# Gate products of the merge stage: three products per weight block run together, their weight sums kept on the chip, operand loads issued by ScalarE

## The chip, the cores and the metric

The kernel runs on one core of one Trainium2 chip. The metric is the time of one execution on the device in microseconds (us). Three runs of the kernel before the change gave 2289.18, 2292.55 and 2293.31 us, median 2292.55 us.

## What is computed

The program is one layer of a hybrid decoder: an input projection, an mLSTM and a sparse attention beside each other, a gated merge of the two, an output projection, cross-attention and a feed-forward block. Only the merge is touched. With `T` = 1056 tokens (1024 of a prompt and 32 of samples) and 1024 channels it is, cut to what matters:

```python
gates = sigmoid(h @ w_gate_m), sigmoid(h @ w_gate_n)      # two gates of 1024 channels
merged = gates[0] * (hm @ w_up_m) + gates[1] * (on @ w_up_n)
```

`h` is the normalised layer input, `hm` the mLSTM's output and `on` the attention's.

## The kernel before, in words

**The gate products.** `merge` (L2237) computes the gate logits by a seven-product scheme for 2x2 blocks (Strassen's in Winograd's form) instead of eight plain products. The weights of each gate are cut into eight blocks `j` of 128 output channels (`N_GATE` = 8; `j // 4` picks the gate), each block into four quarters of 128x512 numbers. The tokens are cut into two halves of 528. The seven products are numbered 1 to 7. Product 1 and 2 use a quarter as it is, 7 the difference of two quarters, 5 the sum of two quarters, 6 is product 5's sum less a third quarter, 3 is the fourth quarter less product 6's sum, 4 a quarter as it is. So 5, 6 and 3 build on each other's weight sums.

**Units.** A unit is one product for one block: 24 fp32r matmuls of 128x128 by 128x264. There are 7 x 8 = 56 units. `GATE_ORDER` is (1, 2, 7, 5, 6, 4, 3): all eight blocks of product 1, then all eight of product 2, and so on. `merge_uses` lists the uses of weights: two of the branch projection (`"m", 0` and `"m", 1`), the 56 units, then the other 14 of the branch projections, which are called late.

**The way of a weight.** For each use, SyncE's queue loads a raw tile (six slots: four `mg_raw`, two in `ring`), VectorE adds or subtracts two quarters if the product wants a sum (`weight_sum`, L2577), ScalarE copies the high part to one of five weight buffers `mg_w` (`weight_high`, L2493), GpSimd forms the low part (L69), and TensorE multiplies. Each product of numbers is three matmuls of high and low parts (`split_product`, L88). A weight buffer is free when the unit that read it is done, so ScalarE can copy at most the weights four units ahead of the one that runs.

**Sums in DRAM.** The raw slots can't hold a sum from product 5 to product 6, eight units later. So SyncE writes each sum of products 5 and 6 to DRAM (`keep_sum`, L2381, tensor `gate_sums`) before it reuses the slot, and loads it again, beside one more quarter, for product 6 (L2368, L2369) and product 3 (L2373, L2374). The reuse of a slot waits on the write (`kept`).

**Operands.** Each product has its own token operand (`B_SOURCE`: from `h_t` or `h_spill` in DRAM, 1056 KB). Three operand buffers `mg_b` rotate. SyncE loads the raw form (`load_b`, L2349) when the product three before is done; ScalarE forms its high part in two pieces (`b_high`, L2509) and VectorE its low part in two (`b_low`, through L69). All of it stands in one order on each engine, written out by the loop over the units.

**Results.** ScalarE copies the results of products 1, 7 and 5 out of PSUM (`keep`, L2504), VectorE adds the others into `mg_za` and `mg_zb` (`evac`, L2593 to L2612). A PSUM pair is free four units later. `gate` (L2514) applies the sigmoid, VectorE then multiplies with the branch projections (`weigh`, L2630).

Of the kernel before, what the change touches and what calls it, by code (L numbers as in the profile page):

```python
# [2222 lines left out]
GATE_ORDER = (1, 2, 7, 5, 6, 4, 3)  # L2223
GATE_QUADS = {1: slice(1, 2), 2: slice(0, 1), 7: slice(1, 3), 5: slice(2, 4), 6: slice(1, 2), 4: slice(3, 4), 3: slice(0, 1)}
N_PAIR, N_GATE = 4, 8


def merge_uses():

    uses = [("m", 0), ("m", 1)] + [(p, j) for p in GATE_ORDER for j in range(N_GATE)]  # L2230
    uses += [("n", 0), ("n", 1)]
    for c in range(2, KD):
        uses += [("m", c), ("n", c)]
    return uses


def merge(nc, A, hm, on, low_at, z_at, b_at, w_at, end, ring, dst_high, dst_low, out_half, tile_at, split_at, psum):  # L2237
# [17 lines left out]
    raw_slot = [4, 4, 5, 5] + [(v - 4) % 6 for v in range(4, LATE)] + [(v - LATE) % 4 for v in range(LATE, NU)]  # L2255
    before = lambda slots, v: max((u for u in range(v) if slots[u] == slots[v]), default=None)
    w_before = [before(w_slot, v) for v in range(NU)]
    raw_before = [before(raw_slot, v) for v in range(NU)]
    parts_of = lambda v: 2 if uses[v][0] in (6, 3) else 1
    raw_count, seen = {}, {}  # L2260
    for v in range(4, NU):
        seen[raw_slot[v]] = seen.get(raw_slot[v], 0) + parts_of(v)
        raw_count[v] = seen[raw_slot[v]]
    kept_count, seen = {}, {}
    for v in range(NU):
        if uses[v][0] in (5, 6):
            seen[raw_slot[v]] = seen.get(raw_slot[v], 0) + 1
            kept_count[v] = seen[raw_slot[v]]
# [3 lines left out]
    Z_ACT = {(p, j): n * N_GATE + j + 1 for n, p in enumerate((1, 7, 5)) for j in range(N_GATE)}  # L2272
    Z_DVE, done = {}, 0
    for p, some in ((2, ("c11",)), (6, ("u2", "u3")), (4, ("u4", "c22", "c21")), (3, ("c12",))):
        for j in range(N_GATE):
            for what in some:
                done += 1
                Z_DVE[what, j] = done
    READ = {2: "c11", 6: "u2", 4: "c21", 3: "c12"}
    B_SOURCE = {1: (0, 0), 2: (4, 0), 3: (4, 1), 5: 0, 7: 1, 6: 2, 4: 3}  # L2280

    with stage(nc, "merge") as (ctx, sem):
# [8 lines left out]
        hm_high, on_high = split_at("mg_hm_high", [P, 4, T], b_at[1]), split_at("mg_on_high", [P, 4, T], b_at[2])  # L2291
# [6 lines left out]
        kept = [sem(f"kept{s}") for s in range(6)]  # L2298
# [4 lines left out]
        def source(v):  # L2303
            if v < 4:
                return raw[4 + v // 2][:, 512 * (v % 2):512 * (v % 2) + 512]
            return raw[raw_slot[v]][:, 0:512]
# [15 lines left out]
        def wait_raw(eng, v):  # L2322
            if v >= 4:
                eng.wait_ge(raw_loaded[raw_slot[v]], 16 * raw_count[v])
# [8 lines left out]
        GATE_READY = {(j // 4, 4 * m + j % 4): n * N_GATE + j + 1 for n, m in enumerate((1, 0)) for j in range(N_GATE)}  # L2333

        @block.sync
        def _(sp):
            def load_b(q):
                s, p = q % 3, GATE_ORDER[q]
                at = B_SOURCE[p]
                if q == 0:  # L2340
                    for k in range(4):
                        sp.dma_start(braw[0][:, k, :], A["h_spill"][:, k, 0:HN]).then_inc(b_first[k], 16)
                    return
                if q < 3:
                    sp.wait_ge(S["up"], 4)
                else:
                    sp.wait_ge(S["prod"], N_GATE * (q - 2))
                src = A["h_t"][at] if isinstance(at, int) else A["h_spill"][:, at[0]:at[0] + 4, half_cols(at[1])]
                sp.dma_start(braw[s][:, :, :], src).then_inc(b_loaded[s], 16)  # L2349

            def load_raw(v):
                u = raw_before[v]
# [4 lines left out]
                x, at = uses[v]  # L2357
                to, done = raw[raw_slot[v]], raw_loaded[raw_slot[v]]
# [4 lines left out]
                quads = A["w_gate"][at // 4, at % 4]  # L2363
                n = GATE_QUADS[x].stop - GATE_QUADS[x].start
                if x == 6:
                    w = unit_use(GATE_ORDER.index(5) * N_GATE + at)
                    sp.wait_ge(kept[raw_slot[w]], 16 * kept_count[w])
                    sp.dma_start(to[:, 0:512], A["gate_sums"][0, at]).then_inc(done, 16)  # L2368
                    sp.dma_start(to[:, 512:1024], quads[:, 1, :]).then_inc(done, 16)  # L2369
                elif x == 3:  # L2370
                    w = unit_use(GATE_ORDER.index(6) * N_GATE + at)
                    sp.wait_ge(kept[raw_slot[w]], 16 * kept_count[w])
                    sp.dma_start(to[:, 512:1024], A["gate_sums"][1, at]).then_inc(done, 16)  # L2373
                    sp.dma_start(to[:, 0:512], quads[:, 0, :]).then_inc(done, 16)  # L2374
                else:
                    sp.dma_start(to[:, 0:512 * n].rearrange("p (q w) -> p q w", q=n), quads[:, GATE_QUADS[x], :]).then_inc(done, 16)
# [6 lines left out]
            load_b(0)  # L2383
            for v in range(4, 8):
                load_raw(v)
            b_at_use = {11: 1, 13: 2}
            for q in range(3, 7):
                b_at_use[N_GATE * (q - 2) + 14] = q
            for v in range(8, LATE):
                if v in b_at_use:  # L2390
                    load_b(b_at_use[v])
                if v >= 10 and v - 6 in kept_count:
                    keep_sum(v - 6)
                load_raw(v)
            for v in range(LATE, LATE + 4):
                load_raw(v)
# [3 lines left out]
            for v in range(LATE + 4, NU):  # L2400
                load_raw(v)
            sp.wait_ge(S["ahead_loaded"], 32)
# [9 lines left out]
        def _(pe):  # L2412
            def up(v, q, x):
                w = wt[w_slot[v]]
                for h in range(2):
                    for c in range(2):
                        g = 2 * h + c
                        if v < FIRST:
                            pe.wait_ge(S["hm_first_low"], g + 1)
                        for k in range(4):  # L2420
                            ks = slice(k * P, (k + 1) * P)
# [7 lines left out]
            def unit(n):  # L2429
                v = unit_use(n)  # L2430
                p, j = uses[v]
                q, s = n // N_GATE, n // N_GATE % 3
# [6 lines left out]
                for c in range(2):  # L2439
                    for k in range(4):  # L2440
                        if n == 0 and c == 0:
# [42 lines left out]
        def _(act):  # L2484
            def weight_high(v):
                wait_raw(act, v)
                if v in sum_count:
                    act.wait_ge(S["w_sum"], sum_count[v])
                if w_before[v] is not None:
# [10 lines left out]
            def keep(n):  # L2500
                p, j = uses[unit_use(n)]
                act.wait_ge(S["prod"], n + 1)
                f, h = {1: (j % 4, 1), 7: (4 + j % 4, 0), 5: (4 + j % 4, 1)}[p]
                nc.scalar.activation(cols(z[j // 4][:, f, half_cols(h)]), pair(n % 4), ACT.Copy).then_inc(S["z_act"], 1)  # L2504
# [19 lines left out]
            for g in range(4):  # L2524
                nc.scalar.activation(bt[1 + g // 2][:, 0, :, col(g % 2)], hm[:, :, col(g)], ACT.Copy).then_inc(S["hm_first_high"], 1)
# [7 lines left out]
            keep_early(1)  # L2533
            weight_high(5)
            for n in range(UNITS):
# [4 lines left out]
                if uses[unit_use(n)][0] in (1, 7, 5):  # L2540
                    keep(n)
                if q < 6 and j in (3, 4):
                    b_high(q + 1, j - 3)
                if q == 6:
                    if j == 0:
                        gate(N_GATE - 1, 1)
                    else:
                        gate(j - 1, 0)
                    if j < 4:
                        other_high(on_high, on, j, N_GATE * 6, "on_high")  # L2550
                    else:
                        other_high(hm_high, hm, j - 4, N_GATE * 5, "hm_high")
                if q == 5 and j:
                    gate(j - 1, 1)
            weight_high(LATE + 2)
            gate(N_GATE - 1, 0)
# [12 lines left out]
        def _(ve):  # L2569
            tt = nc.vector.tensor_tensor  # L2570

            def weight_sum(v):
                x, j = uses[v]
                wait_raw(ve, v)
                w = raw[raw_slot[v]]
                a, b = w[:, 0:512], w[:, 512:1024]
# [2519 lines left out]
```

## Time and profile before

| what | value |
|---|---|
| median of three runs | 2292.55 us (2289.18 to 2293.31) |
| the profiled execution's own time | 2294.28 us |
| its span in the profile | 2292.1 us |
| granted clock of TensorE, mean | 0.968 of full speed |
| TensorE busy | 2166.3 us, 95% of the span |
| VectorE, ScalarE, GpSimd busy | 1355.2, 906.7, 640.8 us |
| the merge stage's matmuls | 840.30 us to 1121.08 us in the span |

Times in the views are microseconds from the start of the span. L88 is the line of every split matmul, L69 that of every low part; there the tile names (`mg_...`) tell the stage. SPq and ACTq are the queues from which SyncE and ScalarE issue DMAs. A clock of 1.00 is TensorE's upper level of 2.4 GHz, 0.50 is 1.2 GHz.

### The profile page before, as it was taken

What the parts mean: (1) busy time and instruction counts of PE and PEld (TensorE: products, weight loads), DVE (VectorE), ACT (ScalarE), POOL (GpSimd) and SP (SyncE); (2) the same over time, 40 slices, a digit from 0 to 9 for tenths busy, and PEclk for the clock granted to TensorE, in tenths of its full rate; (3) what the DMA queues carried; (4) which work ended last, traced back from release to release, by engine and by line L of the source; (5) the groups of instructions that cost most, each with busy time, mean ns of one, the idle gap of its engine ahead of it and who ended that gap; (6) DMA issues with size and microseconds to landing.
All of it is one profiled execution on the core that took longest, in us unless ns stands there. A gap on an engine that the chain in (4) does not pass through costs nothing. (4 is left out here: it accounts for less than half of the span.)

```text
span 2292.1 us, 44079 instructions
## 1 busy us (share of the span) xinstructions
PE 2166.3 (95%) x17491; PEld 1982.6 (86%) x17491; DVE 1355.2 (59%) x2442; ACT 906.7 (40%) x1806; POOL 640.8 (28%) x562
## 2 busy tenths in 40 slices
PE   9999998989888989979999999999899999999997
PEld 7799977865555679979999988898899999999997
DVE  2323445256665664466428145657899887876957
ACT  4221244116655654343234133554333433334443
POOL 0000025412232214432111300132344433445643
PEclk9999999879999999989999999999999999999998
DMA  4231187973453436551221146342223132265234
GB/s 152 105 116 47 36 156 243 308 280 112 139 167 93 146 118 214 168 170 56 83 87 37 38 187 238 122 140 84 89 94 117 72 121 89 85 234 186 91 120 147
DMA packets 147593, 302.87 MB, mean 132 GB/s; under 512 B 26211, under 2 KB 78084, under 8 KB 141693
## 3 DMA queue, kind: packets, MB, share of 16 engines
q1 hardware_dynamic: 124668, 258.77, 33.8%
q0 software_dynamic: 10368, 28.33, 3.9%
q10 hardware_dynamic: 12352, 12.96, 1.8%
q8 instruction: 139, 2.28, 0.4%
q14 instruction: 66, 0.53, 0.1%
HBM read 247.41 MB, written 56.78 MB: 133 GB/s over the span
## 5 line engine op out<-in xcount | busy, mean ns | idle before, releaser
L88 PE MATMUL psum<-mg_b,mg_w 128*128 128x264 f32 x1440 | 183.8, 291 | 18.9 <-DVE mg_b L69 10.2
L88 PEld LDWEIGHTS psum<-mg_b,mg_w 128*128 128x128 f32 x1440 | 182.6, 195 | 20.1 <-issue 17.6
L88 PE MATMUL psum<-merged_high,oq_half 128*128 128x352 f32 x768 | 188.7, 326 | 1.8 <-POOL oq_half L69 1.4
L88 PE MATMUL psum<-ff_t,ff_x_slots 128*128 128x264 f32 x1200 | 149.1, 284 | 1.4 <-DVE ff_x_slots L69 1.4
L88 PEld LDWEIGHTS psum<-ff_t,ff_x_slots 128*128 128x128 f32 x1200 | 147.1, 188 | 1.6 <-issue 1.5
L88 PEld LDWEIGHTS psum<-merged_high,oq_half 128*128 128x128 f32 x768 | 135.2, 190 | 2.5 <-POOL oq_half L69 1.9
L1662 POOL DMA_DIRECT2D na_kv<-in_pool x128 | 69.0, 539 | 230.8 <-PE psum L1869 160.3
L1967 ACT ACTIVATE na_pt<-psum 128x512 f32<-128x512 f32 (+1 forms) x170 | 86.6, 543 | 93.5 <-PE psum L1842 85.0
L88 PE MATMUL psum<-ff_bslot,ff_x_slots 128*128 128x264 f32 x888 | 117.8, 286 | 0.7 <-DVE ff_z L4599 0.7
L69 POOL TENSOR_TENSOR ff_x_slots<-low,ff_x_slots 128x512 fp32r<-128x512 f32 x52 | 82.2, 1594 | 113.8 <-ACT ff_x_slots L4047 108.9
L88 PEld LDWEIGHTS psum<-ff_bslot,ff_x_slots 128*128 128x128 f32 x888 | 112.5, 189 | 1.0 <-DVE ff_z L4599 0.9
L88 PE MATMUL psum<-ff_t,ff_slot 128*128 128x264 f32 x840 | 106.5, 287 | 5.8 <-DVE ff_bufs L4476 2.2
L88 PEld LDWEIGHTS psum<-ff_t,ff_slot 128*128 128x128 f32 x840 | 104.6, 191 | 6.4 <-DVE ff_bufs L4476 2.4
L1842 PEld LDWEIGHTS psum<-consts,na_p 128*128 128x128 f32 x528 | 59.7, 148 | 54.6 <-DVE na_p L2116 31.1
L69 POOL TENSOR_TENSOR mg_w<-mg_raw,mg_w 128x512 fp32r<-128x512 f32 x50 | 73.6, 1479 | 112.0 <-ACT mg_w L2493 111.9
L88 PE MATMUL psum<-ff_b,ff_x_slots 128*128 128x264 f32 x840 | 104.8, 284 | 0.0
L88 PEld LDWEIGHTS psum<-ff_b,ff_x_slots 128*128 128x128 f32 x840 | 103.2, 188 | 0.0
L88 PE MATMUL psum<-in_half,h_high 128*128 128x512 f32 (+3 forms) x360 | 101.0, 366 | 2.2 <-DVE in_half L69 2.2
L1947 ACT ACTIVATE na_p<-na_p,na_nm 128x640 f32<-128x640 f32 (+7 forms) x128 | 92.8, 727 | 25.7 <-DVE na_nm L1983 25.5
L88 PE MATMUL psum<-ff_b,ff_slot 128*128 128x264 f32 x744 | 97.5, 290 | 3.6 <-DVE ff_bufs L4486 2.1
L88 PE MATMUL psum<-x_half_high,ff_aw 128*128 128x264 f32 x512 | 96.9, 288 | 3.4 <-DVE h_again_low L69 3.4
L88 PEld LDWEIGHTS psum<-ff_b,ff_slot 128*128 128x128 f32 x744 | 94.6, 194 | 4.2 <-DVE ff_bufs L4486 2.5
(692 smaller groups left out, 5457.6 us busy)
## 6 DMA issues: line engine op xcount, KB each, us to landing
na_kv<-in_pool SPq DMA_DIRECT2D x128, 128.0 KB, 3.6
na_kv<-in_pool POOLq DMA_DIRECT2D x128, 128.0 KB, 4.2
ff_bslot_raw<-mid_ops SPq DMA_DIRECT2D x59, 264.0 KB, 3.2
mid_ops<-ff_bufs SPq DMA_DIRECT2D x11, 1056.0 KB
ring<-in_f_wu SPq DMA_DIRECT2D x11, 1024.0 KB, 5.3
low<-in_f_wg SPq DMA_DIRECT2D x22, 512.0 KB, 4.6
first_pages<-in_pool SPq DMA_DIRECT2D x68, 128.0 KB, 5.8
ff_wd<-in_f_wd SPq DMA_DIRECT2D x3, 2816.0 KB, 11.6
```

The costliest lines, as they stand in the source:

```text
L69: return engine.tensor_tensor(low, x, high.bitcast(F32), ALU.subtract)
L88: ins = nc.tensor.matmul(out, w[a], x[b], start=first and n == 0, stop=last and n == 2)
L1662: eng.dma_start(kv[m % 2][:, b, 2 * PAGE * p:2 * PAGE * (p + 1)], A["pool"][ds(g, 1), :, 2 * PAGE:4 * PAGE].rearrange("a p x -> (a p) x")) ...
L1842: last = nc.tensor.transpose(out[:, c:c + P], src, K["ident"][:, :])
L1947: ins = nc.scalar.activation(x, x, ACT.Exp, bias=nm[:, b, g, i:i + 1], scale=-1.0, accum_out=sums[:, b, g:g + 1])
L1967: nc.scalar.activation(dst, psum[:, 4 + n % 2, 0:2 * m * P], ACT.Copy).then_inc(S["copied"], 1)
```

## The change

It reorders the units: products 1 and 2 as before, then products 5, 6 and 3 mixed block by block (`SHARED`), then 7 and 4. The four quarters of a block come in two loads of 512 KB, "sums" and "last"; product 5's sum, product 6's and product 3's are formed in these two slots one after the other. `gate_sums` and its 16 writes and 16 reads are gone. The operand loads of all products but the first move from SyncE's queue to ScalarE's. Results are added in another order (ScalarE keeps products 1 and 5 alone, VectorE takes 7), VectorE forms the weight sums five units ahead instead of four, the sigmoids of the first gate half move to product 7's units, a product's first unit waits for its operand in two steps, and the very first operand piece is formed in two halves.

```diff
-GATE_ORDER = (1, 2, 7, 5, 6, 4, 3)
+GATE_ORDER = (1, 2, 5, 6, 3, 7, 4)
+SHARED = [(p, j) for j in range(3) for p in (5, 6)] + [(3, 0), (3, 1)]
+SHARED += [x for j in range(3, 6) for x in ((5, j), (6, j), (3, j - 1))]
+SHARED += [(5, 6), (5, 7), (6, 6), (6, 7), (3, 5), (3, 6), (3, 7)]
+GATE_QUADS = {1: slice(1, 2), 2: slice(0, 1), 7: slice(1, 3), 4: slice(3, 4), "sums": slice(2, 4), "last": slice(0, 2)}
...
+def merge_loads(uses):
+    loads, seen = [], set()
+    for v in range(4, len(uses)):
+        p, j = uses[v]
+        if p not in (5, 6, 3):
+            loads.append(uses[v])
+        elif j not in seen:
+            seen.add(j)
+            loads += [("sums", j), ("last", j)]
+    return loads
...
+    first_parts = [(0, slice(0, 2)), (0, slice(2, 4)), (1, slice(0, 4)), (2, slice(0, 4)), (3, slice(0, 4))]
...
+            def load_raw(n):
+                x, at = loads[n]
+                u = load_before[n]
                 if u is not None:
-                    if u in kept_count:
-                        sp.wait_ge(kept[raw_slot[u]], 16 * kept_count[u])
-                    wait_w_low(sp, u)
+                    p, j = loads[u]
+                    if p == "sums":
+                        wait_w_low(sp, use_of[6, j])
+                        sp.wait_ge(S["w_sum"], sum_count[use_of[3, j]])
+                    else:
+                        wait_w_low(sp, use_of[3, j] if p == "last" else use_of[p, j])
...
-            def keep_sum(v):
-                x, j = uses[v]
-                sp.wait_ge(S["w_sum"], sum_count[v])
-                sp.dma_start(A["gate_sums"][0 if x == 5 else 1, j], raw[raw_slot[v]][:, 0:512]).then_inc(kept[raw_slot[v]], 16)
...
-                        elif j == 0 and k == 0:
-                            pe.wait_ge(S["b_low"], 4 + 2 * q)
+                        elif j == 0 and c == 0 and k % 2 == 0:
+                            pe.wait_ge(S["b_low"], 4 + 2 * (q - 1) + k // 2 + 1)
...
+            def load_b(q):
+                s, p = q % 3, GATE_ORDER[q]
+                at = B_SOURCE[p]
+                if q < 3:
+                    act.wait_ge(S["up"], 4)
+                else:
+                    act.wait_ge(S["prod"], unit_of[GATE_ORDER[q - 3], N_GATE - 1] + 1)
+                src = A["h_t"][at] if isinstance(at, int) else A["h_spill"][:, at[0]:at[0] + 4, half_cols(at[1])]
+                act.dma_start(braw[s][:, :, :], src).then_inc(b_loaded[s], 16)
...
+            b_load_at, b_high_at = {9: 3, 17: 4, 35: 5, 38: 6}, {3: 1, 10: 2, 13: 3, 19: 4, 37: 5, 43: 6}
             for n in range(UNITS):
                 q, j = divmod(n, N_GATE)
                 v = n + 6
                 if v < LATE + 2:
                     weight_high(v)
-                if uses[unit_use(n)][0] in (1, 7, 5):
+                if GATE_UNITS[n] in Z_ACT:
                     keep(n)
-                if q < 6 and j in (3, 4):
-                    b_high(q + 1, j - 3)
+                if n in b_load_at:
+                    load_b(b_load_at[n])
+                if n in b_high_at:
+                    b_high(b_high_at[n], 0)
+                if n - 1 in b_high_at:
+                    b_high(b_high_at[n - 1], 1)
+                if q == 5:
+                    gate(j, 0)
...
             for n in range(UNITS):
                 q, j = divmod(n, N_GATE)
-                v = unit_use(n + 4)
+                v = unit_use(n + 5)
                 if v in sum_count:
                     weight_sum(v)
                 evac(n)
...
-           "h_t": (4, P, 4, T // 2), "gate_sums": (2, 8, P, 512)}
+           "h_t": (4, P, 4, T // 2)}
```

SyncE's queue before, in the middle of product 5's and 6's units (`mg_b_raw_13002` is the raw operand of one product, 128x2112 numbers; `mg_raw_...` and `ring` are raw weight slots):

```order
L2368 DMA mg_raw_12986<-gate_sums 128x512
L2369 DMA mg_raw_12986<-in_w_gate 128x512
L2349 DMA mg_b_raw_13002<-h_t 128x2112
L2381 DMA gate_sums<-ring 128x512
L2368 DMA ring<-gate_sums 128x512
L2369 DMA ring<-in_w_gate 128x512
L2381 DMA gate_sums<-ring 128x512
L2368 DMA ring<-gate_sums 128x512
```

The same queue now, in the units of products 5, 6 and 3:

```order
L2376 DMA mg_raw_12985<-in_w_gate 128x1024
L2376 DMA mg_raw_12986<-in_w_gate 128x1024
L2376 DMA ring<-in_w_gate 128x1024 x2
L2376 DMA mg_raw_12983<-in_w_gate 128x1024
L2376 DMA mg_raw_12984<-in_w_gate 128x1024
```

A write, a read of a sum and a load of a quarter per unit, with an operand load among them, have become loads of 512 KB alone, two for three units.

ScalarE's order now, in the units around product 3's first one (`mg_w_...` are weight buffers, `mg_b_12998` and `mg_b_raw_13001` product 3's operand, L2500 its load):

```order
L2479 ACTIVATE mg_w_12991<-mg_raw_12983 128x512
L2500 DMA mg_b_raw_13001<-h_spill 128x4x528
L2479 ACTIVATE mg_w_12992<-mg_raw_12986 128x512
L2490 ACTIVATE mg_za<-psum 128x528
L2479 ACTIVATE mg_w_12988<-ring 128x512
L2505 ACTIVATE mg_b_12998<-mg_b_raw_13001 128x1056
L2479 ACTIVATE mg_w_12989<-mg_raw_12985 128x512
L2490 ACTIVATE mg_za<-psum 128x528
L2505 ACTIVATE mg_b_12998<-mg_b_raw_13001 128x1056
```

The operand's load (issued from SyncE before) now stands between ScalarE's weight copies, and its two high parts follow behind it in the same order.

## Rows read from the trace of the kernel before

**Rows 1.** The page's head and section 1: span, then busy time by engine.

```profile
span 2292.1 us, 44079 instructions
PE 2166.3 (95%) x17491; PEld 1982.6 (86%) x17491; DVE 1355.2 (59%) x2442; ACT 906.7 (40%) x1806; POOL 640.8 (28%) x562
```

**Rows 2.** Windows: stretch, length, busy us (instructions) of PE PEld DVE ACT POOL, clock, DMA, GB/s.

```profile
858.00:873.00 15.00, 15.00 (x125) 15.00 (x125) 2.52 (x2) 7.59 (x12) 8.01 (x6) 1.00 0.54 182
873.00:890.00 17.00, 17.00 (x142) 17.00 (x141) 3.37 (x5) 5.14 (x8) 7.23 (x6) 1.00 0.72 248
...
1008.00:1023.00 15.00, 9.48 (x58) 9.31 (x57) 11.13 (x16) 8.71 (x11) 7.41 (x5) 0.77 0.31 99
```

**Rows 3.** TensorE's waits, 836 to 1126 us: total, times, longest.

```profile
PE psum L88 <- DVE mg_b L69: 10.2, 3, 5.5
PE psum L88 <- POOL mg_w L69: 8.7, 4, 5.1
```

**Rows 4.** Timeline of TensorE, gate products: start, length, idle before and its releaser.

```profile
840.30 121.25 PE L88 MATMUL psum<-mg_b,mg_w 128*128 128x264 f32 x984 [3.32 <-DVE mg_b L69]
...
977.40 11.90 PE L88 MATMUL psum<-mg_b,mg_w 128*128 128x264 f32 x96 [1.34 <-DVE mg_b L69]
994.44 13.76 PE L88 MATMUL psum<-mg_b,mg_w 128*128 128x264 f32 x96 [5.14 <-POOL mg_w L69]
1013.72 25.96 PE L88 MATMUL psum<-mg_b,mg_w 128*128 128x264 f32 x192 [5.52 <-DVE mg_b L69]
1039.52 0.28 PE L88 MATMUL psum<-mg_on_high,mg_w 128*128 128x264 f32 x1
```

**Rows 5.** Timeline of ScalarE: copies of product 1's first and eighth result.

```profile
856.70 0.61 ACT L2504 ACTIVATE mg_za<-psum 128x528 f32<-128x528 f32 x1 [1.26 <-PE psum L88]
...
877.10 0.61 ACT L2504 ACTIVATE mg_zb<-psum 128x528 f32<-128x528 f32 x1 [1.79 <-PE psum L88]
```

**Rows 6.** Windows of TensorE alone, after the last long wait: length, busy, clock, DMA.

```profile
1014.00:1017.00 3.00, 3.00 (x15) 0.50 0.15 57
```

**Rows 7.** Timeline of SyncE's queue, issues around two of the operand loads.

```profile
942.53 0.32 SPq L2349 DMA_DIRECT2D mg_b_raw<-h_t  x1
942.91 0.42 SPq L2381 DMA_DIRECT2D gate_sums<-ring  x1
951.01 0.32 SPq L2368 DMA_DIRECT2D ring<-gate_sums  x1
...
980.59 0.43 SPq L2349 DMA_DIRECT2D mg_b_raw<-h_spill  x1
981.07 0.50 SPq L2381 DMA_DIRECT2D gate_sums<-mg_raw  x1
989.26 0.33 SPq L2376 DMA_DIRECT2D mg_raw<-in_w_gate  x1
```

**Rows 8.** DMAs, issues of 836 to 1126 us: KB each, median us to landing.

```profile
mg_raw<-in_w_gate SPq DMA_DIRECT2D x10, 512.0 KB, 5.0
mg_b_raw<-h_t SPq DMA_DIRECT2D x4, 1056.0 KB, 7.7
```

**Rows 9.** DMAs, issues of 879 to 890 us: the slowest landings of 512 and 1056 KB.

```profile
mg_b_raw<-h_t SPq DMA_DIRECT2D x1, 1056.0 KB, 8.6
mg_raw<-in_w_gate SPq DMA_DIRECT2D x2, 512.0 KB, 6.5
```

**Rows 10.** Tiles mg_raw, mg_b: ns min/median/max of one, first and last start.

```profile
L2493 ACT ACTIVATE mg_w<-mg_raw x50: 612/623/636, 849.0 to 1101.5; 128x512 fp32r<-128x512 f32 x50
L69 POOL TENSOR_TENSOR mg_w<-mg_raw,mg_w x50: 1262/1294/2297, 850.4 to 1102.9; 128x512 fp32r<-128x512 f32 x50
L2577 DVE TENSOR_TENSOR mg_raw<-mg_raw x20: 677/692/1786, 889.4 to 1019.9; 128x512 f32<-128x512 f32 x20
L69 DVE TENSOR_TENSOR mg_b<-mg_b_raw,mg_b x16: 696/1255/2352, 845.7 to 1012.0; 128x1056 fp32r<-128x1056 f32 x12, 128x528 fp32r<-128x528 f32 x4
L2509 ACT ACTIVATE mg_b<-mg_b_raw x12: 1066/1076/1078, 866.0 to 1003.4; 128x1056 fp32r<-128x1056 f32 x12
```

More of the change, by code:

```diff
@@ L2264, in merge @@
[L2264 to L2268, printed above, removed]
+    loads = merge_loads(uses)
+    late_load = loads.index(uses[LATE])
+    load_slot = [n % 6 for n in range(late_load)] + [(n - late_load) % 4 for n in range(late_load, len(loads))]
+    load_before = [before(load_slot, n) for n in range(len(loads))]
+    load_count = [load_slot[:n + 1].count(load_slot[n]) for n in range(len(loads))]
@@ L2269, in merge @@
+    load_of = {}
+    for v in range(4, NU):
+        p, j = uses[v]
+        load_of[v] = loads.index(("sums", j) if p in (5, 6) else ("last", j) if p == 3 else (p, j))
     summed = [v for v in range(NU) if uses[v][0] in (7, 5, 6, 3)]
     sum_count = {v: n + 1 for n, v in enumerate(summed)}
-    Z_ACT = {(p, j): n * N_GATE + j + 1 for n, p in enumerate((1, 7, 5)) for j in range(N_GATE)}
+    use_of = {x: v for v, x in enumerate(uses)}
+    unit_of = {x: v - FIRST for v, x in enumerate(uses)}
@@ L2273, in merge @@
+    kept_units = [x for x in GATE_UNITS if x[0] in (1, 5)]
+    Z_ACT = {x: n + 1 for n, x in enumerate(kept_units)}
     Z_DVE, done = {}, 0
[L2274 to L2279, printed above, removed]
+    for p, j in GATE_UNITS:
+        for what in {1: (), 2: ("c11",), 5: (), 6: ("u2", "u4"), 3: ("c12",), 7: ("u3", "c22"), 4: ("c21",)}[p]:
+            done += 1
+            Z_DVE[what, j] = done
@@ L2297, in merge @@
         raw_loaded = [sem(f"raw_loaded{s}") for s in range(6)]
-        kept = [sem(f"kept{s}") for s in range(6)]
         b_first = [sem(f"b_first{k}") for k in range(4)]
@@ L2362, in load_raw @@
                     return
[L2363 to L2376, printed above, removed]
-            def keep_sum(v):
-                x, j = uses[v]
-                sp.wait_ge(S["w_sum"], sum_count[v])
-                sp.dma_start(A["gate_sums"][0 if x == 5 else 1, j], raw[raw_slot[v]][:, 0:512]).then_inc(kept[raw_slot[v]], 16)
[L2383 to L2396, printed above, removed]
+                quads = A["w_gate"][at // 4, at % 4][:, GATE_QUADS[x], :]
+                some = GATE_QUADS[x].stop - GATE_QUADS[x].start
+                sp.dma_start(to[:, 0:512 * some].rearrange("p (q w) -> p q w", q=some), quads).then_inc(done, 16)
+            for k in range(4):
+                sp.dma_start(braw[0][:, k, :], A["h_spill"][:, k, 0:HN]).then_inc(b_first[k], 16)
+            for n in range(late_load + 4):
+                load_raw(n)
             for j in range(2):
@@ L2399, in _ @@
                 sp.dma_start(ring[:, j, :], A["w_out"][j]).then_inc(S["ahead_loaded"], 16)
-            for v in range(LATE + 4, NU):
-                load_raw(v)
+            for n in range(late_load + 4, len(loads)):
+                load_raw(n)
             sp.wait_ge(S["ahead_loaded"], 32)
@@ L2522, in part_high @@
                 nc.scalar.activation(dst_high[:, c, :], za[:, c, :], ACT.Copy).then_inc(S["parts_high"], 1)
-            for g in range(4):
-                nc.scalar.activation(bt[1 + g // 2][:, 0, :, col(g % 2)], hm[:, :, col(g)], ACT.Copy).then_inc(S["hm_first_high"], 1)
+            for g, ks in first_parts:
+                nc.scalar.activation(bt[1 + g // 2][:, 0, ks, col(g % 2)], hm[:, ks, col(g)], ACT.Copy).then_inc(S["hm_first_high"], 1)
             weight_high(2)
@@ L2572, in weight_sum @@
             def weight_sum(v):
[L2573 to L2576, printed above, removed]
-                tt(a, a, b, ALU.add if x == 5 else ALU.subtract).then_inc(S["w_sum"], 1)
+                p, j = uses[v]
+                if p == 6:
+                    first, last = (raw[load_slot[loads.index((x, j))]] for x in ("sums", "last"))
+                    ve.wait_ge(S["w_sum"], sum_count[use_of[5, j]])
+                    wait_load(ve, loads.index(("last", j)))
+                    tt(first[:, 512:1024], first[:, 0:512], last[:, 512:1024], ALU.subtract).then_inc(S["w_sum"], 1)
+                elif p == 3:
+                    first, last = (raw[load_slot[loads.index((x, j))]] for x in ("sums", "last"))
+                    ve.wait_ge(S["w_sum"], sum_count[use_of[6, j]])
+                    tt(last[:, 0:512], last[:, 0:512], first[:, 512:1024], ALU.subtract).then_inc(S["w_sum"], 1)
+                else:
+                    w = raw[load_slot[load_of[v]]]
+                    wait_load(ve, load_of[v])
+                    tt(w[:, 0:512], w[:, 0:512], w[:, 512:1024], ALU.add if p == 5 else ALU.subtract).then_inc(S["w_sum"], 1)
             def b_low(q, m):
@@ L2662, in _ @@
                 evac(n)
-                if q < 6 and j in (4, 6):
-                    b_low(q + 1, (j - 4) // 2)
+                if n in b_low_at:
+                    b_low(b_low_at[n], 0)
+                if n - 1 in b_low_at:
+                    b_low(b_low_at[n - 1], 1)
                 if q == 6 and 1 <= j <= 4:
```

110 lines of the change are left out of this document (47 added, 63 removed).

## The prediction

> **What bounds the kernel now.** I read the page's head first: TensorE is busy for 95% of a span of 2292.1 us [rows 1]. So only its idle time and its slow time can be won. The windows say where in the merge it is slow. From 858 to 890 us it does 125 matmuls in 15 us and 142 in 17, about 0.12 us each, at clock 1.00; from 1008 to 1023 only 58, at clock 0.77 [rows 2]. The list of TensorE's waits names two releasers, `mg_b` from VectorE for 10.2 us and `mg_w` from GpSimd for 8.7 us, 18.9 us together [rows 3].
>
> The timeline gives the stage's ideal. Product 1's first result is copied at 856.70 us and its eighth at 877.10, seven units later: a unit takes 2.914 us [rows 5]. Unit 0 thus began at about 853.8 us, and the last of the 56 ended at 1039.5, where the first `mg_on_high` matmul stands [rows 4]. That is 185.7 us; 56 units of 2.914 us are 163.2. **22.5 us are lost.** Of these 18.9 less the 3.32 us that stand before the first matmul, so 15.6 us, are idle [rows 3, 4]. The other 6.9 us are slow matmuls: after each long wait TensorE runs at 1.2 GHz for some time, 15 matmuls in 3 us at clock 0.50 where 25 are usual [rows 6].
>
> SyncE's queue shows what is late. At 942.53 us it issues an operand load, right behind it the write of a sum to DRAM, and the next read of a sum into that slot waits for this write until 951.01, 8.1 us later. The same again: operand load at 980.59, write at 981.07, next weight load at 989.26 [rows 7]. TensorE idles 5.14 us before 994.44 for that weight. The 5.52 us before 1013.72 are put down to the operand's low part [rows 4], but VectorE's low part stands in its order behind the weight sums, which wait for the reads of `gate_sums`. So nearly all comes from the round trip of the sums and from what stands behind it in an order.
>
> **The change, part by part.** I call E(n) the end of unit n.
>
> *Round trip removed.* 16 writes and 16 reads of 256 KB and the waits on them go. At most 22.5 us come back, at least 0. What is late next is either a weight or an operand, so I check both.
>
> *Weights in the mixed stretch.* A weight buffer is free at E(n-1) for unit n+4. ScalarE copies 0.62 us, GpSimd takes 1.29, at most 2.30 [rows 10]: ready by E(n-1)+2.9, needed at E(n+3), 11.7 us after E(n-1). The raw slot "last" of block 0 is free when unit 22's low part is done, at E(17)+2.9 at the latest. SyncE issues (0.4 us) and 512 KB land in 5.0, at most 6.5 us [rows 8, 9]: E(17)+9.8. Then sum, high and low part, at most 1.79+0.62+2.30: E(17)+14.5. Unit 25 needs it at E(24), which is E(17)+20.4. Later blocks have the same distance or more. Slack 6 us, so no stall: 0. Traffic: 1 MB per three units (8.7 us) is 120 GB/s, 512 KB per unit in product 7 is 180; the old stretch of product 7 moved 248 GB/s while TensorE never idled [rows 2].
>
> *Other engines.* Per three units VectorE has three sums (0.69) and three result additions (0.70): 4.2 of 8.7 us. GpSimd has 1.29 of 2.9. ScalarE loses eight result copies and gets six DMA issues of about 0.43 us. None is near its limit. The queue behind ScalarE's waits is its weight copies, which have 8 us of lead: cost 0. If that cover went, each microsecond would show on TensorE.
>
> *Operands.* Six loads go to ScalarE's order. Two are tight. Product 3's (needed by unit 22, second step 0.73 us after E(21)): its second high part follows the result copy of unit 20, so E(20)+0.6+1.07, then the low part 1.25, at worst 2.35 [rows 10]: ready at E(20)+2.9 to 4.0, needed at E(20)+3.6. Stall 0 to 0.4 us. Product 7's: issued just after E(34), lands 7.7, at most 8.6 us later [rows 8, 9]. Two high parts with a weight copy between them need 2.8 us, the low part 1.25 to 2.35, so done at 11.7 to 13.8 us after E(34). On VectorE it also stands behind the result of unit 38, which makes it E(38)+0.7+1.25 to 2.35, so 13.6 to 14.7. Needed at E(39)+0.7, which is 15.3. Slack 0.6 to 1.7 us; the load itself may take up to about 10.5 us. Stall 0 as shown, 3 us if it lands 3 us later than any did. I take 0.8 us for all operands together, near the lower end, since the rows' medians leave slack.
>
> The rows say that an operand load on SyncE's queue held up what stood behind it for 8 us [rows 7]. A second queue lets the weights go on beside it. The Trainium skill (DMA: Bandwidth & Descriptors, "Issuing engines are not separate DMA queues") speaks against a gain from this part: loads from ScalarE run on the same 16 engines and interleave, so only issue time is saved. By that rule the 1056 KB take as long as before and the weights beside them longer, and this part alone gives back about 0.4 us for each of six loads on SyncE, none of it on TensorE. My sum does not need the part: 22.5 us is the whole loss, from whatever queue.
>
> *The start.* The first operand piece is made in two halves, so ScalarE's 1.07 and VectorE's 1.25 us shrink to about 0.6 and 0.7 [rows 10] before the first matmul; but VectorE first splits a weight. The first matmul comes about 0.5 us earlier and the following pieces 0.1 later. Between 0 and 1.2 us; I take 0.3.
>
> *The end.* The 16 late products and the following stage find the same orders behind them, their rows show TensorE busy, and they move up with it: 0.
>
> **Sum:** 22.5 + 0.3 - 0.8 = 22.0 us. The profiled execution took 2294.28 us, so 2272.3 by its own measure. It stands 1.7 us above the median of 2292.55, so I forecast **2270.5 us** against the median. The likeliest case alone: from a loss of 3.5 us that stays (2273.5) to all 22.5, 1.2 at the start and a run on the low side by some 2 us (2267).
>
> **Rivals.** *A: a late operand takes the place (0.16).* Product 7's or product 3's load meets the weight loads on the other queue and lands after 11 us. For: 0.6 us of slack at worst. Against: none took over 8.6 us. Its price is that of the stretch from 1008 to 1023 us, where 58 matmuls took 15 us instead of 7: 8 us with the slow clock [rows 2]. Gain 14, **2278.5 us**. The page's rule points this way too.
>
> *B: weights stay late in part (0.11).* Waits that I put down to the round trip are in truth bandwidth: 512 KB loads then land late in the mixed stretch and in product 7's, and half the loss stays. Against: 248 GB/s went without a stall. Gain 11, **2281.5 us**.
>
> *C: slower (0.05).* ScalarE is one order: while it waits at its high part for an operand, the weight copies of all later units stand behind it. This decides once a load takes more than the 10.5 us and also eats the weights' lead of 8 us, so from about 19 us, over twice the slowest row. Then each of five loads stops TensorE for the 5.5 us seen at 1013.72 and slows it as there, 8 us each: 40 us lost, 22.5 won, **2310 us**.
>
> *D: the change does not do what it says (0.02).* The stalls come back at full length elsewhere in the stage, at the first wait for an operand or in what follows. **2292.5 us.**
>
> **How the numbers follow.** Forecast 0.66, A 0.16, B 0.11, C 0.05, D 0.02. About 0.2%, 4.6 us, is what a measurement of this kernel can tell from no change. Forecast, A and B are all faster by more: 0.93. Same 0.02, slower 0.05. The range goes from 2267 us to 2279.5, which takes in A and leaves out B, C and D, 0.18.
>
> **What would show it.** The list of waits in the merge has 4 to 5 us instead of 18.9, nearly all before the first matmul, and no entry over 1 us after it. The clock is 1.00 in every window from unit 4 to the end of the gate products. `mg_on_high` begins near 1017 us instead of 1039.5, and everything later is 22 us earlier. No `gate_sums` rows. `mg_b` loads of 1056 KB stand on ScalarE's queue and land in 7 to 9 us. Wrong would be: a wait for `mg_b` of over 2 us at unit 22 or unit 40 (A), waits for `mg_w` in the mixed units (B), ScalarE idle for long on a DMA of `mg_b_raw` with TensorE idle behind it (C), or a stage shorter by 22 us with the span not shorter by as much (D).

## The result and the profile after

| | before | after |
|---|---|---|
| median | 2292.93 us (2289.18 to 2294.81, 4 runs) | 2264.78 us (2262.45 to 2267.57, 4 runs) |
| profiled execution's own time, span | 2294.28, 2292.1 us | 2262.45, 2260.8 us |
| mean granted clock | 0.968 | 0.975 |
| merge's first matmul to the first `mg_on_high` matmul | 840.3 to 1039.5 us | 833.0 to 1009.8 us |

The ratio of the time after to the time before is 0.988, with an interval of 0.9862 to 0.9898: 23.4 to 31.6 us faster. The forecast was 2270.5 us, its range 2267 to 2279.5. The measured median lies 2.2 us below the range.

The page's head and section 1 of the kernel after, against [rows 1]: TensorE does the same 17491 matmuls in 14.5 us less of busy time, and its idle time shrinks too.

```profile
span 2260.8 us, 44015 instructions
PE 2151.8 (95%) x17491; PEld 1971.8 (87%) x17491; DVE 1359.1 (60%) x2443; ACT 904.5 (40%) x1799; POOL 646.7 (29%) x562
```

TensorE's waits after, 830 to 1126 us (total, times, longest), against [rows 3]:

```profile
PE psum L88 <- DVE mg_b L69: 2.7, 1, 2.7
PE psum L88 <- PEq L146: 0.3, 1, 0.3
```

Of 18.9 us one wait of 2.7 is left, and the timeline of TensorE shows that it stands before the first matmul. With the 0.3 us of the second row that is 3.0, where the prediction had 4 to 5. The six gaps inside the units before, of 0.4 to 5.5 us (three of them in [rows 4]), are gone; the row of 1435 matmuls (from a window that begins at 834 us, so inside the row above it) has no gap in it.

```profile
829.96 0.33 PE L1853 MATMUL psum<-consts,na_acc 128*128 128x128 f32 x1
833.03 17.17 PE L88 MATMUL psum<-mg_b,mg_w 128*128 128x264 f32 x124 [2.74 <-DVE mg_b L69]
...
833.72 176.23 PE L88 MATMUL psum<-mg_b,mg_w 128*128 128x264 f32 x1435
1009.79 0.28 PE L88 MATMUL psum<-mg_on_high,mg_w 128*128 128x264 f32 x1
```

ScalarE's timeline has the copy of an early result (`mg_early`) that is released as TensorE turns to unit 0, at 846.8 us. From there to 1009.8 are 163.0 us; 56 units of 2.914 us are 163.2. Nothing is lost in the units any more.

```profile
846.85 0.61 ACT L2484 ACTIVATE mg_early<-psum 128x528 f32<-128x528 f32 x1 [2.31 <-PE psum L88]
```

The windows say the same of the clock (columns as in [rows 2]): 1.00 everywhere but at the start, busy as long as the window is.

```profile
833.03:850.00 16.97, 16.92 (x124) 16.71 (x125) 8.58 (x10) 9.71 (x17) 6.74 (x5) 0.90 0.61 194
...
890.00:922.00 32.00, 32.00 (x266) 32.00 (x265) 26.80 (x26) 11.53 (x18) 19.88 (x12) 1.00 0.44 150
922.00:960.00 38.00, 38.00 (x315) 38.00 (x314) 26.97 (x28) 12.29 (x19) 20.96 (x14) 1.00 0.51 177
960.00:990.00 30.00, 30.00 (x250) 30.00 (x249) 22.43 (x27) 18.59 (x23) 15.05 (x11) 1.00 0.33 115
```

Where the rest of the 31.3 us between the two spans comes from needs more profiles than two. The experiments give eleven more, so one table stands here for all. "Stage" runs from the start of the last attention matmul (L1853) to the first `mg_on_high` matmul; "rest" from there to the end of the span. All in us.

| kernel | attention ends | stage | rest | span |
|---|---|---|---|---|
| before | 836.6 | 202.9 | 1252.6 | 2292.1 |
| before, again (`e1_before_again`) | 833.8 | 202.0 | 1252.7 | 2288.5 |
| `e5_before_operands_on_act` | 833.3 | 199.0 | 1255.0 | 2287.3 |
| `e11_before_low_first` | 834.1 | 200.0 | 1252.5 | 2286.6 |
| after | 830.0 | 179.8 | 1251.0 | 2260.8 |
| after, again (`e2_after_again`) | 832.8 | 179.8 | 1250.8 | 2263.4 |
| `e3_tensor_declared` | 836.1 | 179.8 | 1250.6 | 2266.5 |
| `e4_operands_on_sync` | 829.7 | 180.4 | 1252.5 | 2262.6 |
| `e6_write_sums_too` | 840.8 | 180.3 | 1249.9 | 2271.0 |
| `e7_start_whole` | 833.4 | 180.1 | 1252.1 | 2265.6 |
| `e8_keep_clock` | 832.2 | 179.8 | 1248.2 | 2260.2 |
| `e9_start_order` | 833.1 | 179.5 | 1251.2 | 2263.8 |
| `e10_start_order_and_clock` | 830.7 | 178.2 | 1252.4 | 2261.3 |

The stage gave 23.1 us in the first pair. Another 6.6 us come from before the merge, where the change touches nothing: the attention ends anywhere from 829.7 to 840.8 us, without regard to the kernel. Between these two extremes, `e4_operands_on_sync` and `e6_write_sums_too`, TensorE's busy time up to the attention's end differs by 9.5 us over as many matmuls, at a mean clock of 0.96 and 0.95, so most of the 11.1 us is slower matmuls and not waiting. The windows of the two (length, busy, clock, DMA, GB/s):

```profile
0.00:829.70 829.70, 768.32 (x6645) 0.96 0.47 148
0.00:840.80 840.80, 777.78 (x6644) 0.95 0.47 146
```

The last 1.6 us are in the rest. They too are a matter of the clock, at one place late in the feed-forward block. 384 matmuls there take 52.5 or 52.6 us in the four profiles of the old order and in that of `e10_start_order_and_clock`, where the clock is at 0.50 for 6.8 us of it, and 50.0 or 50.1 us in the eight others, where it stays at 1.00. In all thirteen TensorE has three short idle times of 0.6 to 0.9 us there. Windows of `before`, `after` and `e10_start_order_and_clock` (columns as above):

```profile
2175.50:2178.50 3.00, 3.00 (x15) 0.50 0.00 0
2145.80:2148.80 3.00, 3.00 (x27) 1.00 0.00 0
2144.90:2147.90 3.00, 3.00 (x16) 0.50 0.01 3
```

This accounts for the 2.2 us by which the rest is shorter on average in the new order (1251.0 against 1253.2): 2.5 us are lost in four of four profiles of the old order and in one of nine of the new. Why the clock fell in some and not in others isn't shown.

### The profile page after: what moved, and what is told of

Read it like the earlier page. It is cut to its first block and busy times, and to the rows that moved or that the text cites. A ratio compares the mean times of both kernels' runs of the same rounds, so it can differ in the third digit from the quotient of the medians.

```text
span 2260.8 us, 44015 instructions
## 1 busy us (share of the span) xinstructions
PE 2151.8 (95%) x17491; PEld 1971.8 (87%) x17491; DVE 1359.1 (60%) x2443; ACT 904.5 (40%) x1799; POOL 646.7 (29%) x562
## 5 line engine op out<-in xcount | busy, mean ns | idle before, releaser
L88 PE MATMUL psum<-mg_b,mg_w 128*128 128x264 f32 x1440 | 176.9, 286 | 2.8 <-DVE mg_b L69 2.7
L88 PEld LDWEIGHTS psum<-mg_b,mg_w 128*128 128x128 f32 x1440 | 176.5, 190 | 3.2 <-DVE mg_w L69 2.9
L69 POOL TENSOR_TENSOR mg_w<-mg_raw,mg_w 128x512 fp32r<-128x512 f32 x51 | 81.6, 1605 | 102.9 <-ACT mg_w L2479 102.8
```

The lines of the kernel that those rows point to most:

```text
L69: return engine.tensor_tensor(low, x, high.bitcast(F32), ALU.subtract)
L88: ins = nc.tensor.matmul(out, w[a], x[b], start=first and n == 0, stop=last and n == 2)
```

## Experiments

**The two kernels once more.** `e1_before_again` is the kernel before, `e2_after_again` the changed one, both without an edit.

> The kernel before, unchanged, as a measure of what two equal programs differ by and of how far the part ahead of the merge moves from one execution to the next. Theory L (luck): the 6.7 us by which the merge began earlier in the changed kernel's profile are spread of the attention stages' clock; then this kernel's merge begins anywhere between about 828 and 840 us, its gate products take 199 us again from first matmul to first late product, and the ratio is 1.000 within 0.002. Theory S (systematic): something in the changed program makes the unchanged stages faster; then the merge begins at 836 us or later here too.

Measured: 2291.9 us (2282.72 to 2298.99, 12 runs) against 2292.46 (2280.65 to 2299.07, 17 runs), ratio 1.0002 (0.9985 to 1.0019). Equal programs differ by up to 18 us between runs. TensorE's waits in this profile:

```profile
PE psum L88 <- DVE mg_b L69: 12.6, 3, 6.5
PE psum L88 <- POOL mg_w L69: 4.6, 5, 1.1
PE psum L88 <- DVE mg_za L2608: 0.9, 1, 0.9
```

The total is that of [rows 3] within 1 us, but its shares are others. Who is named at a wait is the last link of one loop, and not a cause by itself.

> The changed kernel, unchanged. Theory L: with more rounds the gain shrinks to that of the merge stage, 22.5 to 24 us, ratio 0.990, and the merge begins anywhere between 828 and 840 us. Theory S: the gain stays at 28 us, ratio 0.988, and the merge begins near 830 us as in the first profile. Both: 176.8 us from the first matmul of the merge to the first late product.

Measured: 2265.03 us (2264.00 to 2269.02, 6 runs), ratio 0.9892 (0.9868 to 0.9916), which is 24.8 us, interval 19.3 to 30.3; the two medians are 27.4 us apart. Both theories' ratios lie in the interval, so the time doesn't decide. The table does as to the stages ahead of the merge: they end between 829.7 and 840.8 us with the new order and between 833.3 and 836.6 with the old, and 840.8 is one of the changed ones. From the first matmul to the first late product there are 176.7 us, as expected. The stage gave 22.2 us in this pair.

**A layout of DRAM?** The tensor `gate_sums` is declared again and stays unused.

```diff
-           "h_t": (4, P, 4, T // 2)}
+           "h_t": (4, P, 4, T // 2), "gate_sums": (2, 8, P, 512)}
```

> The changed kernel with the DRAM tensor gate_sums declared but not used, so that DRAM is laid out as before. Theory S in the form that the layout of DRAM helps the other stages: the gain falls from 28 to about 22.5 us (ratio 0.990) and the merge begins at 836 us. Theory L: no different from the changed kernel within 2 us.

Measured: 2265.68 us (2261.88 to 2273.97), ratio 0.9895 (0.9866 to 0.9923), stage 179.8. The declaration changes nothing that these runs can tell.

**Operands back on SyncE's queue, in the new order.** `load_b` moves from ScalarE to SyncE unchanged but for the engine.

```diff
+            b_before = {7: 1, 9: 2, 16: 3, 20: 4, 35: 5, 37: 6}
...
+                if n in b_before:
+                    load_b(b_before[n])
...
-                if n in b_load_at:
-                    load_b(b_load_at[n])
```

> The changed kernel with the six operand loads back on SyncE's queue, before the weight loads that are released at about the same time. My theory, that the round trip was the loss and the second queue gives nothing of it: the same time within 2 us, no wait over 1 us for mg_b or mg_w in the units. Rival, that the second queue carries a good part of the gain since weights stood behind operand loads: weights land up to 8 us later at three places, and 5 to 12 us come back as waits for mg_w or mg_b.

Measured: 2267.97 us (2264.25 to 2271.07), ratio 0.9904 (0.9880 to 0.9928), stage 180.4. The second queue is worth 0.6 us of the stage here. The 2.9 us between this median and that of `e2_after_again` are not in any wait, and the intervals overlap.

**Operands on ScalarE's queue, in the old order.** The converse. The loads are issued once the product three before is done. That is also earlier than before, where they stand in SyncE's order: product 4's at 926.17 us instead of 942.53, product 3's at 955.23 instead of 980.59. So the edit moves both the queue and the time of the loads.

```diff
+            load_b(1)
             weight_high(5)
+            load_b(2)
...
+                if j == 1 and 1 <= q < 5:
+                    load_b(q + 2)
```

> The kernel before with one part of the change alone: its six operand loads issued by ScalarE; products in the old order, sums through DRAM as before. My theory, that the waits come from the round trip as such and from the order that puts a sum's write, read and use close together: at most a third of the loss goes, the merge's gate products still take over 190 us from the first matmul to the first late product (176.7 in the changed kernel, 198.3 to 199.2 before), with waits for mg_w and mg_b of over 10 us beside the start. Rival, that what hurt was the write of a sum standing behind a 1056 KB operand load in one queue: the writes then land in about 4 us instead of 8.1, the waits before 961, 971 and 994 us go, and 10 us or more come back.

Measured: 2285.95 us (2280.20 to 2293.42, 12 runs) against 2293.62 (17 runs), ratio 0.9968 (0.9956 to 0.9981), 4.4 to 10.1 us. The stage takes 199.0 us, 3.0 to 3.9 less. TensorE's timeline, to be held against [rows 4]:

```profile
964.69 3.17 PE L88 MATMUL psum<-mg_b,mg_w 128*128 128x264 f32 x24 [3.22 <-POOL mg_w L69]
971.10 5.62 PE L88 MATMUL psum<-mg_b,mg_w 128*128 128x264 f32 x24 [3.23 <-POOL mg_w L69]
977.07 23.66 PE L88 MATMUL psum<-mg_b,mg_w 128*128 128x264 f32 x192 [0.35 <-DVE mg_b L69]
1007.18 25.26 PE L88 MATMUL psum<-mg_b,mg_w 128*128 128x264 f32 x192 [6.45 <-DVE mg_b L69]
```

In the stage the gain is under a third of the 22.5 us, as the theory said. The wait of 5.14 us at 994 is gone, two of 3.2 have come earlier, and the longest stays. Of what went, the part of the queue and that of the earlier loads can't be told apart: the write that stood beside an operand load at 981.07 us [rows 7] goes out at 979.85 now, with none beside it. The queue did not spare a write that runs beside an operand load. Here are the landings of what was issued from 925 to 930 us, then of what was issued from 930 to 945 us (KB each, median us):

```profile
mg_b_raw<-h_t ACTq DMA_DIRECT2D x1, 1056.0 KB, 7.7
gate_sums<-mg_raw SPq DMA_DIRECT2D x1, 256.0 KB, 8.3
...
gate_sums<-mg_raw SPq DMA_DIRECT2D x2, 256.0 KB, 3.3
```

Beside a load of 1056 KB on the other queue 256 KB took 8.3 us, as long as on the load's own queue [rows 7]; with no operand load beside them the next ones took 3.3. The Trainium skill (DMA: Bandwidth & Descriptors, "Issuing engines are not separate DMA queues") says that DMAs issued from different engines share the same 16 hardware engines; by it another queue doesn't spare the write. This trace agrees for the write; the load landed in 7.7 us, the median of [rows 8], and was not late.

**The writes put back into the new order.** All 16 sums are written out again by SyncE, and the slot's next load waits for them. Nothing is read back.

```diff
                     if p == "sums":
+                        for i, x in enumerate((5, 6)):
+                            sp.wait_ge(S["w_sum"], sum_count[use_of[x, j]])
+                            sp.dma_start(A["gate_sums"][i, j], raw[load_slot[u]][:, 512 * i:512 * i + 512]).then_inc(kept, 16)
+                        sp.wait_ge(kept, 32 * (j + 1))
```

> The changed kernel with the 16 writes of the sums to DRAM put back, and with SyncE's wait on them before it reloads the slot; nothing is read back. If the write and the wait on it were the cost, 5 us or more come back as waits for mg_w. My theory is that a wait of 4 to 8 us fits in the distance of three blocks that the new order leaves between a slot's use and its reload: within 2 us of the changed kernel, no new wait over 1 us.

Measured: 2265.86 us (2261.21 to 2272.68), ratio 0.9885 (0.9866 to 0.9905), stage 180.3. TensorE's waits and, in the second fence, the writes' landings (KB each, median us):

```profile
PE psum L88 <- DVE mg_b L69: 2.9, 2, 2.7
```

```profile
gate_sums<-mg_raw SPq DMA_DIRECT2D x10, 256.0 KB, 5.7
...
gate_sums<-ring SPq DMA_DIRECT2D x6, 256.0 KB, 5.9
```

Sixteen writes of 5.7 us with a wait behind each pair cost 0.5 us of the stage at most. So the writes and their waits are not dear by themselves. That they were dear in the old order because it left no room for them is read from the traces, above all [rows 7]; the old order without them wasn't run.

**VectorE's order in the kernel before.** In the kernel before, the low part of the operand goes ahead of the sum and of the result in each turn of the loop.

```diff
+                if q < 6 and j in (4, 6):
+                    b_low(q + 1, (j - 4) // 2)
                 if v in sum_count:
                     weight_sum(v)
                 evac(n)
-                if q < 6 and j in (4, 6):
-                    b_low(q + 1, (j - 4) // 2)
```

It starts from VectorE's timeline in the kernel before, ahead of the wait at 1013.72:

```profile
989.41 0.70 DVE L2608 TENSOR_TENSOR mg_za<-mg_za,psum 128x528 f32<-128x528 f32 x1 [0.48 <-PE psum L88]
1000.88 0.69 DVE L2577 TENSOR_TENSOR ring<-ring 128x512 f32<-128x512 f32 x1 [10.76 <-DMA ring<-in_w_gate]
...
1011.99 1.59 DVE L69 TENSOR_TENSOR mg_b<-mg_b_raw,mg_b 128x1056 fp32r<-128x1056 f32 x1
```

VectorE stands for 10.8 us before a sum whose quarters were loaded late, then works off what has piled up, the low part last.

> The kernel before with one edit: VectorE forms an operand's low part ahead of the weight sum and the result additions of the same unit instead of behind them. The longest wait of the kernel before (5.5 and 6.5 us, ahead of product 3's first unit) is put down to this low part. If its place behind one unit's sum and additions is the cause, the wait goes. My theory is that VectorE is late because it stood still for 10.8 us at a sum that waited for its load from DRAM, and works off six units: then the wait shrinks by the 3.1 us of one unit's work and 2 to 3 us stay, and the ratio is 0.998 to 1.000.

Measured: 2287.47 us (2280.58 to 2294.16, 12 runs), ratio 0.9980 (0.9965 to 0.9996), stage 200.0. TensorE's timeline, then VectorE's, at the same place:

```profile
992.50 13.44 PE L88 MATMUL psum<-mg_b,mg_w 128*128 128x264 f32 x96 [3.54 <-POOL mg_w L69]
1009.20 3.13 PE L88 MATMUL psum<-mg_b,mg_w 128*128 128x264 f32 x16 [3.27 <-DVE mg_b L69]
```

```profile
1000.29 1.49 DVE L69 TENSOR_TENSOR mg_b<-mg_b_raw,mg_b 128x1056 fp32r<-128x1056 f32 x1 [10.53 <-ACT mg_b L2509]
```

The longest wait before product 3's first unit fell from 5.5 and 6.5 us to 3.3, near the 2 to 3 us of the theory, but by another path: VectorE stands now before the low part itself, for 10.5 us. The rest stays since ScalarE is late as well: its high part of the operand stands behind the copies of the weights that SyncE issued 8 us late. ScalarE's timeline of this kernel shows the idle time before two of them:

```profile
990.38 0.63 ACT L2493 ACTIVATE mg_w<-mg_raw 128x512 fp32r<-128x512 f32 x1 [8.15 <-DMA mg_raw<-in_w_gate]
994.24 0.63 ACT L2493 ACTIVATE mg_w<-mg_raw 128x512 fp32r<-128x512 f32 x1 [3.23 <-DMA mg_raw<-in_w_gate]
```

**The first operand piece whole.** In the changed kernel the two halves become one again.

```diff
-    first_parts = [(0, slice(0, 2)), (0, slice(2, 4)), (1, slice(0, 4)), (2, slice(0, 4)), (3, slice(0, 4))]
+    first_parts = [(0, slice(0, 4)), (1, slice(0, 4)), (2, slice(0, 4)), (3, slice(0, 4))]
...
```

> The changed kernel with the first operand piece formed in one instead of two halves. Expected by my sum: the first matmul comes 0.5 to 0.6 us later after the end of the stage before (3.65 us instead of 3.07), and the first late product 0.3 us later: within 1 us of the changed kernel. Rival: the halves cost as much as they give, and the stage is not longer.

Measured: 2269.30 us (2265.03 to 2274.82, 4 runs), ratio 0.9905 (0.9880 to 0.9930). The first matmul stands 3.65 us after the last attention matmul instead of 3.07, but the stage is only 0.3 us longer.

**The clock at the start, and VectorE's order there.** `e8_keep_clock` fills TensorE's idle time before the merge with matmuls whose result nobody reads. `e9_start_order` makes VectorE split the second weight behind the last of the operand pieces. `e10_start_order_and_clock` has both edits, in the changed kernel each.

```diff
+            for _ in range(4):
+                nc.tensor.matmul(psum[:, 7, 0:HG], hm[:, 0, 0:P], hm[:, 1, 0:HG], start=True, stop=True)
...
-                if g == 1:
+                if g == 3:
```

> The changed kernel with four fp32 matmuls of 128x264 on hm at the merge's start, whose results nobody reads, in the time in which TensorE waits for its first operand. In the changed kernel the first 124 matmuls take 17 us at a mean clock of 0.90, where full speed would take 15. If the idle time ahead of the stage is what drops the clock, unit 0 begins about 2 us earlier after the end of the stage before (14.8 instead of 16.8 us), and the kernel gains 2 us. Rival: the clock falls for what the attention's last microseconds look like, or the four are too few; then nothing changes, and nothing is lost.

> The changed kernel with VectorE splitting the second branch weight after the fourth operand piece instead of after the second. In the profile of the run with the clock kept up, TensorE waited for the later pieces; here the clock is low at the start as in the changed kernel. If VectorE's order bounds the start whatever the clock, unit 0 begins 1 us earlier after the end of the stage before (15.8 us instead of 16.8). If the slow clock bounds it, nothing changes.

Windows of TensorE alone (length, busy, clock, DMA), of the changed kernel first, then of `e8_keep_clock`:

```profile
834.00:836.00 2.00, 2.00 (x12) 0.53 1.01 289
836.00:838.00 2.00, 2.00 (x13) 0.62 0.80 233
```

```profile
836.00:838.00 2.00, 2.00 (x17) 1.00 0.91 254
838.00:840.00 2.00, 1.49 (x13) 1.00 0.96 276
```

The clock is kept at 1.00, yet the stage takes 179.8 us as without the edit. The timeline of `e8_keep_clock` shows why: the faster TensorE now waits for VectorE's low parts.

```profile
833.40 2.02 PE L2453 MATMUL psum<-low 128*128 128x264 f32 x8 [0.83 <-PEq L146]
835.32 3.42 PE L88 MATMUL psum<-mg_b,mg_w 128*128 128x264 f32 x24
839.24 1.74 PE L88 MATMUL psum<-mg_b,mg_w 128*128 128x264 f32 x12 [0.51 <-DVE mg_b L69]
841.51 8.76 PE L88 MATMUL psum<-mg_b,mg_w 128*128 128x264 f32 x70 [0.53 <-DVE mg_b L69]
```

Times: 2265.89 us (2261.86 to 2275.32) for `e8_keep_clock`, 2266.15 (2263.38 to 2268.38) for `e9_start_order`, whose stage is 0.3 us shorter.

> Both edits of the start, the four matmuls that keep the clock and VectorE's other order. If each hides the other's bound, the two together bring what neither does alone: unit 0 at 15 us or less after the end of the stage before, 1.5 to 2 us less than 16.8, and the fastest median of all. If VectorE's low parts bound the start in any order (two of them take over 2 us beside GpSimd), 16.3 us or more.

Measured: 2263.37 us (2260.79 to 2270.74, 6 runs), ratio 0.9883 (0.9859 to 0.9907). Each edit alone gave 0 and 0.3 us of the stage, both together 1.6, the 1.5 to 2 us expected (unit 0 begins 15.3 us after the last attention matmul, not at 15 or less). The first matmuls run without a gap:

```profile
831.83 2.02 PE L2453 MATMUL psum<-low 128*128 128x264 f32 x8 [0.83 <-PEq L146]
833.75 22.50 PE L88 MATMUL psum<-mg_b,mg_w 128*128 128x264 f32 x181
```

It is the lowest median of all, but 1.7 us below that of `e2_after_again` is less than runs of one kernel differ by. Only the stage's time shows it.

## Why the prediction was right in its mechanism and wrong in its range

- **The loss of 22.5 us** comes back, as far as two pairs of profiles can tell, whole. The stage is 23.1 and 22.2 us shorter in two pairs of profiles, against 22.0 forecast, and units 0 to 55 take 163.0 us.
- **The round trip as its cause.** Right as to the place, but too coarse. `e6_write_sums_too` has the writes and the waits for them and loses 0.5 us. What the traces show as late is a write that has to be finished one turn of the queue later, while an operand load beside it more than doubles its time (8.3 against 3.3 us), with ScalarE's and VectorE's orders behind it. The mixed order spares this by distance: sums are used where they lie. The part of the 16 reads and of the extra quarters wasn't measured apart, and the new order with sums read back wasn't tried, so how the 22.5 us divide between the reads and the order stays open.
- **Weights: no stall forecast, none seen.** The 512 KB loads took 4.0 us in `mg_raw` and 6.2 in `ring`, against 5.0 in `mg_raw` [rows 8] and 3.9 in `ring` before. Those in `ring` were slower than before, and still TensorE waited for none. The 248 GB/s that the prediction ascribes to the old stretch of product 7 [rows 2] were moved ahead of it, while TensorE had the last units of product 1 and the first of product 2.
- **Operands: 0.8 us forecast, 0 seen.** Product 3's low part was the tight one, as said: done at 910.9 us, needed by about 911.6. VectorE's timeline has one of its two parts at nearly the worst length of [rows 10]:

```profile
906.53 2.34 DVE L69 TENSOR_TENSOR mg_b<-mg_b_raw,mg_b 128x1056 fp32r<-128x1056 f32 x1
...
909.64 1.26 DVE L69 TENSOR_TENSOR mg_b<-mg_b_raw,mg_b 128x1056 fp32r<-128x1056 f32 x1 [0.17 <-ACT mg_b L2505]
```

  Product 7's operand landed in 7.6 us. ScalarE waited 0.98 us for it, and its low part was done at 963.2 us, some 0.8 before its use:

```profile
948.90 0.33 ACTq L2500 DMA_DIRECT2D mg_b_raw<-h_t  x1
...
956.52 1.09 ACT L2505 ACTIVATE mg_b<-mg_b_raw 128x1056 fp32r<-128x1056 f32 x1 [0.98 <-DMA mg_b_raw<-h_t]
```

- **The start: 0.3 us forecast.** The first matmul comes 0.58 us earlier after the attention's end, unit 0 by 0.3 (`e7_start_whole`).
- **Rivals A to D** did not come. The slacks held by a little under 1 us, so A was near. The second queue, on which the prediction's sum did not rest, gives 0.6 us in the new order. In the old one it gave 3 to 4 in the stage together with the earlier issue of the loads, where the prediction had 0 on TensorE for this part. Which of the two brought them isn't shown.
- **The step that failed is the low end of the range**, "all 22.5, 1.2 at the start and a run on the low side by some 2 us (2267)", and behind it a term put at nothing, "The end": 0. It isn't one lucky measurement: the changed kernel's median is 2264.78, 2265.03 again (`e2_after_again`), and 2265.68 with a tensor declared. Nor was the base off: 67 runs of the kernel before have a median of 2292.5. The mean of these 67 less that of ten runs of the changed kernel (2292.2 and 2265.5) is 26.7 us, an estimate good to about 2 us, where 22.0 were forecast. Of this the stage gave 22.7, and the rest of the span 2.2, where the forecast had 0: TensorE's clock in one stretch of the feed-forward block, as shown above. Another 0.5 us lies outside the span: the time of a run is 2.2 us longer than its span in the kernel before and 1.7 in the changed one, on average; no run shows why. The remaining 1.3 us is within the spread.
- **The allowance for runs** was too small as well. Equal programs come out between 2280.65 and 2299.07 us (67 runs of the kernel before, standard deviation 4.0 us), and the attention alone ends up to 11 us apart over the thirteen profiles. Three runs within 4.1 us of each other had looked like a spread of 4.

## What to carry to other kernels

Before you price a transfer on a path, ask how far in the order its result lies from its use, and what stands behind the wait on each engine: the old order, with each write waited for one turn of the queue later and each sum fetched again, lost 22 us in this kernel; the same writes cost 0.5 at most where the slot's next load was three blocks away. Read a gain from the time between two events of the stage that was changed, and size the range from the spread of that difference and of the whole program's runs apart. Where two small limits lie at one place, take both away before calling either harmless.

## What was not expected of the hardware

- The part ahead of the merge, the same in all thirteen profiles, ends between 829.7 and 840.8 us, most of it slower matmuls (busy 768.3 and 777.8 us). Single runs of the kernel before differ by 18 us.
- Late in the feed-forward block, with the same three idle times of 0.6 to 0.9 us in all thirteen profiles, TensorE's clock fell to 0.50 for 6.8 us in five of them and stayed at 1.00 in eight. It made a difference of 2.5 us.
- A write of 256 KB took 8.3 us beside a load of 1056 KB issued by another engine, 3.3 us with none beside it.
- After about 3 us of idling TensorE's clock was 0.53 and 0.62 in the next two windows of 2 us. Eight instructions of 128x264 in 2.02 us ahead of the real ones kept it at 1.00. That alone gave nothing in the stage (179.8 us with and without it): VectorE's low parts then stopped TensorE twice, for 0.5 us each. With VectorE's order changed too it was 178.2.
